# Latent attention: scores and maxima two tiles ahead, three transposed tiles in a ring, value products two steps behind

## The reference

```python
def mla_mixer(h, w_in, q_norm_g, kv_norm_g, w_uq, w_ukv, w_out, cos, sin):
    proj = h @ w_in
    c_q, c_kv, k_rope, g = split(proj)                       # 256, 128, 64, 2048 columns
    q = (rmsnorm(c_q, q_norm_g) @ w_uq)                      # 16 heads x (128 + 64)
    kv = (rmsnorm(c_kv, kv_norm_g) @ w_ukv)                  # 16 heads x (128 + 128)
    for i in range(S // 128):                                # 8 tiles of 128 queries
        q0, k_end = i * 128, (i + 1) * 128
        s = (q_nope[q0:k_end] . k_nope[:k_end] + q_rope[q0:k_end] . k_rope[:k_end]) * scale
        p = softmax(where(causal, s, -inf))                  # over i + 1 blocks of 128 keys
        outs.append(p @ v[:, :k_end])
    return (o * silu(g)) @ w_out
```

## Time and profile before

| | |
|---|---|
| median of 3 timed runs | 2548.24 us (2547.0 to 2550.31) |
| the profiled execution, own time | 2545.83 us |
| its span, first to last instruction | 2544.1 us |
| mean granted TensorE clock | 0.979 |
| PE busy | 2343.1 us, 92% |
| DVE busy | 1572.1 us, 62% |
| ACT busy | 1338.4 us, 53% |
| POOL busy | 486.3 us, 19% |

### The profile page before, as it was taken

The page is one execution under the profiler, slowest core; times in us unless marked ns, Lnnn a source line. Parts: engine busy times, 40 slices in busy tenths (PEclk is TensorE's granted clock), DMA queues, the critical chain, the costliest instruction groups (busy, mean ns, idle before and its releaser), DMA issues. The chain is left out here.

```text
span 2544.1 us, 43259 instructions
## 1 busy us (share of the span) xinstructions
PE 2343.1 (92%) x17364; PEld 1324.1 (52%) x17364; DVE 1572.1 (62%) x2220; ACT 1338.4 (53%) x2013; POOL 486.3 (19%) x434
## 2 busy tenths in 40 slices
PE   8999998988788888988897899999999999999987
PEld 4667663444444445544453455554555446776643
DVE  5566675776656656655566566666665665667764
ACT  4444443445554445454543677777778643444442
POOL 0000111122112011111032133322332520011011
PEclk9999999998899999999999999999999999999999
DMA  3011112214333334343341211112111221111013
GB/s 118 26 43 43 42 37 89 73 48 83 75 79 80 87 65 90 72 90 77 91 102 52 65 43 49 52 51 59 43 46 39 75 68 35 40 46 34 35 61 122
DMA packets 198682, 160.32 MB, mean 63 GB/s; under 512 B 160306, under 2 KB 163122, under 8 KB 198484
## 3 DMA queue, kind: packets, MB, share of 16 engines
q1 hardware_dynamic: 194388, 153.36, 22.6%
q0 software_dynamic: 4096, 4.20, 0.7%
HBM read 98.79 MB, written 4.19 MB: 40 GB/s over the span
## 5 line engine op out<-in xcount | busy, mean ns | idle before, releaser
L240 PE MATMUL psum<-h_hi,w_hi 128*128 128x512 f16 x1128 | 429.9, 381 | 35.7 <-ACT mla_silu_g L285 18.5
L242 PE MATMUL psum<-h_hi,w_lo 128*128 128x512 f16 x1128 | 429.8, 381 | 0.0
L241 PE MATMUL psum<-h_lo,w_hi 128*128 128x512 f16 x1128 | 429.5, 381 | 0.0
L2408 DVE SCALAR_TENSOR_TENSOR w_lo<-wf,w_hi 128x1024 f16<-128x1024 f32 (+3 forms) x194 | 233.5, 1212 | 137.0 <-ACT w_hi L2403 137.0
L256 PE MATMUL psum<-w_hi,h_hi 128*128 128x128 f16 x1504 | 258.0, 220 | 0.0
L257 PE MATMUL psum<-w_lo,h_hi 128*128 128x128 f16 x1504 | 257.6, 220 | 0.0
L258 PE MATMUL psum<-w_hi,h_lo 128*128 128x128 f16 x1504 | 257.5, 220 | 0.0
L1681 ACT ACTIVATE ssum<-psum,mla_neg_top 128x128 f32<-128x128 f32 (+7 forms) x128 | 94.7, 740 | 298.3 <-DVE mla_neg_top L1588 298.3
L1140 POOL TENSOR_TENSOR sb_al<-sb_zc,sb_ah 128x256 f16<-128x256 f32 (+2 forms) x96 | 166.7, 1736 | 372.2 <-ACT sb_ah L1102 372.2
L2403 ACT ACTIVATE w_hi<-wf 128x1024 f16<-128x1024 f32 (+3 forms) x194 | 187.1, 975 | 41.9 <-PE psum L242 24.5
L240 PEld LDWEIGHTS psum<-h_hi,w_hi 128*128 128x128 f16 x1128 | 110.6, 98 | 156.6 <-issue 39.7
(11 more groups left out here) (332 smaller groups left out, 5839.5 us busy)
## 6 DMA issues: line engine op xcount, KB each, us to landing
wf<-in_gla_out SPq DMA_DIRECT2D x32, 512.0 KB, 3.5
wf<-in_sb_in SPq DMA_DIRECT2D x32, 512.0 KB, 3.5
wf<-in_mla_out SPq DMA_DIRECT2D x20, 512.0 KB, 3.6
wf<-in_gla_v SPq DMA_DIRECT2D x16, 512.0 KB, 3.5
wf<-in_gla_g SPq DMA_DIRECT2D x16, 512.0 KB, 3.5
wf<-in_mla_gate SPq DMA_DIRECT2D x16, 512.0 KB, 3.8
wf<-in_sb_out SPq DMA_DIRECT2D x16, 512.0 KB, 3.5
xT<-in_x_T SPq DMA_DIRECT2D x16, 256.0 KB, 5.3
```

The source lines that it names most:

```text
L240: pe.matmul(out, wh[:, w], act_hi[:, k, tok], start=(i == 0), stop=False)
L241: pe.matmul(out, wh[:, w], act_lo[:, k, tok], start=False, stop=False)
L242: mm = pe.matmul(out, wl[:, w], act_hi[:, k, tok], start=False, stop=(i == last))
L2408: dve.scalar_tensor_tensor(out=self.w_lo[s % Layer.NSPLIT][:, 0:cols], in0=self.wf[s % Layer.NLOAD][:, 0:cols], scalar=W_SCALE, in1=self.w ...
```

## The change

The loop of the latent layer is put in another order. Scores and maximum of a tile are listed two tiles ahead instead of one. The exponential becomes an item of its own, `e`, behind the division `d` of the tile before it. The value product is listed two steps behind instead of one, right behind the scores, and the gap that stood between them moves behind it. The prologue does scores and maximum of tiles 0 and 1. The two buffers of transposed tiles become one of 21 x 256 columns, in which each tile takes what its width needs, at a place given by a table; a transpose waits for the value product of tile t - 3 instead of t - 2. The buffers of the high and low halves before the transpose stay two. No arithmetic changes.

```diff
--- before.py
+++ after.py
@@ -1209,7 +1209,7 @@
             self.qr = sb("qr_stack", [P, 4, T], F16)
             self.prob = net.ssum
             self.ph = [sb(f"prob_halves{i}", [P, 2 * T], F16) for i in range(2)]
-            self.pt = [sb(f"prob_halves_T{i}", [P, 2 * T], F16) for i in range(2)]
+            self.pt = sb("prob_halves_T", [P, self.TURNED * 2 * P], F16)
             self.cq_hi, self.cq_lo = sb("cq_hi", [P, 2, T], F16), sb("cq_lo", [P, 2, T], F16)
             self.ckv_hi, self.ckv_lo = sb("ckv_hi", [P, 1, T], F16), sb("ckv_lo", [P, 1, T], F16)
             self.kr_hh, self.kr_ll = sb("kr_hh", [P, T], F16), sb("kr_ll", [P, T], F16)
@@ -1228,7 +1228,7 @@
             self.cm = [t[:].bitcast(F32) for t in self.ph]
             self.cr = [yh[:, 3 * T:4 * T], yl[:, 3 * T:4 * T]]
 
-            self.kt = [t[:].bitcast(F32)[:, c * HALF:(c + 1) * HALF] for t in self.pt for c in range(2)]
+            self.kt = [self.pt[:].bitcast(F32)[:, i * HALF:(i + 1) * HALF] for i in range(4)]
 
             self.gate, self.split = Gate(L), Split(L)
             self.resid = Residual(L, [self.rt[0][:], self.rt[1][:]], pool_half=0,
@@ -1266,6 +1266,7 @@
     END = [("gu", 0, 0), ("gw", 2), ("gu", 0, 1), ("gu", 1, 0), ("ns", 1)] + [("nk", 1, k) for k in range(KD)] + [
         ("gu", 1, 1), ("gu", 2, 0), ("gu", 2, 1), ("gu", 3, 0), ("gu", 3, 1), ("gl", 3), ("gl", 4)]
     OUT_CLOSES = 5
+    TURNED, TURNED_AT = 21, (20, 12, 15, 8, 0, 15, 8, 0)
     ORDER = "uuuuuugrgr", "uuguuguuxrxrxx"
     def pe_cost(self, item):
 
@@ -1360,7 +1361,7 @@
         items += [("w", s) for s in range(3, 7)]
         L.split_early = range(4, 1000)
         last = MLA_HEADS * TT - 1
-        items += [("s", 0), ("m", 0), ("d", 0)]
+        items += [("s", 0), ("m", 0), ("e", 0), ("s", 1), ("m", 1), ("d", 0), ("e", 1)]
         main, filler = [], []
         for t in range(last + 1):
             h, i = divmod(t, TT)
@@ -1373,13 +1374,15 @@
             elif i == TT - 1 and h + 1 < MLA_HEADS:
                 items += weave_even(main, L.cut(filler, ("x", "g")), self.pe_cost)
                 main, filler = [], []
-            main += [("s", t + 1), ("m", t + 1), ("gap", 1)] if t < last else []
-            main += [("pv", t - 1)] if t else []
+            main += [("s", t + 2), ("m", t + 2)] if t + 2 <= last else []
+            main += [("pv", t - 2)] if t >= 2 else []
+            main += [("gap", 1)]
             main += [("d", t + 1)] if t < last else []
+            main += [("e", t + 2)] if t + 2 <= last else []
             if h % 2 and h + 1 < MLA_HEADS and 1 <= i < 5:
                 main += self.stage_items(h + 1, range(2 * i - 2, 2 * i))
             main += [("gap", 1)]
-        main += [("gap", 2), ("pv", last)]
+        main += [("pv", last - 1), ("gap", 2), ("pv", last)]
         items += weave_even(main, filler, self.pe_cost)
         early, tail = L.open_early(L.cut(self.last_out(1), ("x",)), 2)
         items += early + [("ns", 0)] + tail
@@ -1417,6 +1420,11 @@
     def gate_out(self, n):
         h, c = self.L.units[n][1]
         return self.sg[:, h % 2, c * HALF:(c + 1) * HALF]
+
+    def turned_at(self, t):
+
+        at = self.TURNED_AT[t % TT] * 2 * P
+        return self.pt[:, at:at + 2 * (t % TT + 1) * P]
 
     def pair(self, t):
 
@@ -1497,7 +1505,7 @@
                 pe.wait_ge(self.yt_ready, t // 4)
             out = L.bank(4)[:, (i % 4) * P:(i % 4 + 1) * P]
             for j in range(i + 1):
-                hi, lo = (self.pt[t % 2][:, k * P:(k + 1) * P] for k in (j, i + 1 + j))
+                hi, lo = (self.turned_at(t)[:, k * P:(k + 1) * P] for k in (j, i + 1 + j))
                 vh, vl = self.v_hi[:, h % 2, j, :], self.v_lo[:, h % 2, j, :]
                 pe.matmul(out, vh, hi, start=(j == 0), stop=False)
                 pe.matmul(out, vl, hi, start=False, stop=False)
@@ -1669,7 +1677,7 @@
             if which == "q" and p >= 1:
                 act.wait_ge(self.stacked[(p - 1) % 2], 256 * ((p - 1) // 2 + 1))
             act.activation(hi, s, ACT.Copy).then_inc(self.rhi, 1)
-        elif kind == "m":
+        elif kind == "e":
             t, = a
             w = (t % TT + 1) * P
             k = slice(t % 4, t % 4 + 1)
@@ -1766,9 +1774,9 @@
             t, = a
             w = (t % TT + 1) * P
             sp.wait_ge(self.pl_ready, t + 1)
-            if t >= 2:
-                sp.wait_ge(self.pv_done, t - 1)
-            sp.dma_start_transpose(self.pt[t % 2][:, 0:2 * w].rearrange("p (j q) -> p j q", q=P),
+            if t >= 3:
+                sp.wait_ge(self.pv_done, t - 2)
+            sp.dma_start_transpose(self.turned_at(t).rearrange("p (j q) -> p j q", q=P),
                                    self.ph[t % 2][:, 0:2 * w]).then_inc(self.turned[t % 2], 16)
 
 
```

## The result

The changed kernel takes 2571.89 us (median of 4 runs, 2569.12 to 2572.58), against 2548.45 us before (4 runs, 2547.0 to 2550.31): a ratio of 1.009, 95% interval 1.0078 to 1.0102. It is 23 us slower where 41 us faster was forecast. The profiled execution has a span of 2570.8 us and a mean granted clock of 0.973.

The account below looks back on a forecast made before the run. PE was taken to bound the kernel, with DVE-ACT pacing heads 0 to 3 about as much. Terms 19.5 + 25.6 - 3.7 = 41.4 us off the profiled 2545.8 gave 2504.4, or 2506.8 us as median; range 2470 to 2541.

Parts of the forecast that it names:

- The removed wait: PE's waits for transposes in the attention loop: all 43.7 us go, 18.1 in heads 0 to 3 and 25.6 after.
- Exponential behind the divisions: In each tile step, the ACT-DVE string of 3.7 us fits 5.6 or 6.3 us; fillers' copies come no later.
- (a): At the gate unit's PSUM bank, the later value product makes no difference; at the ends 1 us a head, 12 us.
- The step on DVE's pace: In heads 0 to 3, DVE's wait for the exponential goes: 178.7 - 18.2 = 160.5 us, for 180.
- The sum by parts: Heads 0 to 3 give 19.5 us, heads 4 to 15 give 25.6, less 3.7 at tile 123: 41.4 us.
- The clock: In heads 0 to 3 the low level costs at most 19.8 us; fewer stops lessen it, capped by DVE.
- (b): Value units of heads 1 to 3: ACT's copy stands an estimated 2.4 us, covered by the earlier exponential.
- (c): Head 15, tile 3 (t = 123): the output unit behind the value product stops PE for 3.1 to 4.3 us, taken as 3.7.
- The other two signs of being wrong: The prediction is wrong if DVE's wait for ACT's high half grows or the untouched layers behind move.
- The rule I set aside: By a skill's example, deeper buffering gains nothing here (2548 us); set aside because 43.7 us of DMA waits remained.
- B: Rival: scores wait for the exponential, over 10 us; gain only 17 us, 2531 us; chance 0.20.
- D: Rival: slower, since ACT's in-order wait for the gated output holds the gate's bank; 2557 at 3.3 us more a head; chance 0.07.

Follow-up runs that it names:

- run 3: The changed kernel, with the planner keeping the gate's copy and the rotary item with their unit when a gap ends between them: 2545.62 us.
- run 9: The changed kernel with only the exponential moved, that of tile t + 1 to the front of step t, behind the maximum of t + 2: 2528.27 us.
- run 8: The changed kernel with the exponential moved to the front of the step, and gate copy and rotary item kept with their unit: 2486.46 us.
- run 1: The kernel before, in its old order, with only the ring of three transposed tiles added: 2548.39 us, ratio 1.0002.
- run 12: run 8 without the look-ahead: scores and maximum one tile ahead, their exponential right behind, value product still two steps behind: 2571.13 us.
- run 2: The changed kernel with the staging items of odd heads listed behind the step's second gap, not in front of it: 2572.07 us.
- 10: run 8 with the last head's output projection opened one step later: 2483.88 us.
- 11: run 10 with the staging items also listed behind the second gap: 2483.20 us.

## Why the prediction was wrong

The changed kernel and the three that differ from it in nothing but the place of the exponential and the kept items put the two causes in a table (medians, us):

| | not kept | kept |
|---|---|---|
| exponential behind the division | 2571.9 (the change) | 2545.6 (run 3) |
| exponential in front | 2528.3 (run 9) | 2486.5 (run 8) |

*The removed wait.* All 43.7 us of waits for the transposes went, as forecast, and the ring by itself costs nothing (run 1), as forecast. That the order was what made the tile late held too.

*The step that failed first: "Exponential behind the divisions".* It was priced at nothing, since the string of 3.7 us fits a step of 5.6 or 6.3 us. The comparison was wrong. Every engine walks the list in its order, so it is not enough that the string fits: for as long as ACT stands in front of the exponential for DVE's low half, no unit's copy behind it frees a bank, and PE has three. The sentence "ACT waits for a low half in place of a maximum, so fillers' copies behind it come no later" compared the length of two waits and not what PE has to do meanwhile. The stop of 3.04 us shown above, 1.04 in run 9, is this case. With the two gaps joined, PE has nothing but units for those banks, but joined gaps are no cost by themselves: run 8 has them too. Moving that one item is worth 43.6 us without the kept items (2571.9 - 2528.3) and 59.1 with them. The look-ahead was under-sized beside this: without it run 8 loses 85 us (run 12) and ACT's wait for the maximum is back. That this wait is what the 85 us are made of is likely and not shown apart.

*The step that failed second: (a), "The gate", "I take no difference".* The bound was 1 us a head either way. Measured are stops of 5.83 and 0.73 us in alternate heads, where before they were 1.8 and 1.4 us, and behind the second gate unit 3.04 and 1.95 us, where before there was one of 0.9 in two heads. By the sums of all gate stops, 70.2 for 23.0 us, that is some 3 us a head more. Two links were missing from the sum, and both come from where the items fall, not from durations. The planner ended its gap between the gate unit and its copy, so the copy came a division and an exponential later; and a rotary copy had slipped behind the staging items, so ACT waited for GpSimd, for which the sum has no term. Keeping them with their unit gives 26.3 us back (run 3) and 41.8 with the exponential in front. The GpSimd link alone, 1.7 us of 5.83, is worth nothing measurable (run 2), and PE's clock is where it went.

*The step on DVE's pace, 178.7 - 18.2 = 160.5 us.* DVE's wait for the exponential did fall, from 18.2 to 1.9 us, but the remaining waits were not constants. They were waits for ACT, and ACT was late for a new reason. A sum of waits by releaser is no budget from which one row can be struck. Nor did 106.5 + 72.2 = 178.7 of 180 us show that DVE set the pace: busy time and waits fill the span of any engine, and PE's 150.4 us busy and 29.4 of waits fill the same 180.

*The sum by parts.* Heads 0 to 3 were to give 19.5 us and gave 7, most of it the shift of the cut. Heads 4 to 15 were to give 25.6 and lost 28 up to tile 120, 18 of standing and 10 of slower work.

*The clock.* I looked for a higher clock in heads 0 to 3 and it came, 0.94 for 0.88 up to tile 32. But it fell from 0.99 to 0.95 where there had been little to lose, and PE's busy time for the same matmuls grew by 10 us there. The term was counted on one side of the change only.

*(b) and (c).* The value units cost a stop of ACT of at most 2.1 us, as covered. The stop behind tile 123 was taken as 3.7 us, between 3.1 and 4.3; it is 3.38. The other two signs of being wrong did not show: DVE's wait for ACT's high half is 119.6 us over the loop, from 120.8, and what comes behind the loop takes the same time within 2 us.

*The rule I set aside.* The ring alone gave 1.0002, with 44.1 us of waits for the transposes still in the loop. So the third tile was no gain by itself, and my answer to the rule, that waits for DMA were still there to be won by depth, was no answer: those waits were the order's. Beside this stands the sentence of the Trainium skill that the prediction cites ("TensorE: Matmul & The Clock Gate", on HAM oscillation), that more buffering gave no further gain; run 1 agrees with its outcome, though not with its premise.

*The rivals.* B, scores waiting for the exponential, was marked at over 10 us: it is there with 12.2 us, nearly all in heads 0 to 3, and is the smaller part. D had the right place, the gate's bank, the right sign and nearly the right price: 3.3 us more a head, against some 3 with the unnamed stops counted in. Its link was only part of it: ACT's wait for the gated product did grow, from 20.5 to 59.5 us, but it was not what came last. It was given 0.07. What none of them had was the three-bank queue behind ACT as a whole. The 44 us of unnamed waits at units are that queue, and runs 8 and 9 show it by making them go (0.7 + 2.4 and 7.2 + 0.7 us inside the loop).

The best orders found, runs 8, 10 and 11, which can't be told apart, are 2.4 to 2.5% faster than the kernel before. Run 8 has the same items as the change, with the exponential in another place and two kinds of items kept with their unit.

## What to carry to other kernels

When an item moves in an in-order queue, the price is not its length against the step, but what stands behind it while it waits, and for how long the consumer of that has other work; here three PSUM banks. After a planner has been fed a changed list, read the list it makes, item by item around each resource that is handed over: gate copies that came an exponential late, some of them cut off from their unit, took 47 us more of PE's time, as much as the removed stall of 43.7. A wait without a named releaser can often be read off the timeline by what ended just before it. And look-ahead and distance are not to be priced one by one: here the same later value product cost 29 us or gained 26.

## What was unexpected of the hardware

Shortening a stop by 1.7 us, from 5.83 to 4.15, in five heads changed the total by nothing (2571.89 and 2572.07 us). Over the loop PE's stops fell by 9.5 us and its busy time rose by 9.6, with a granted clock of 0.94 for 0.95.

Where it went can be seen. In both kernels PE also stands 3.04 us behind each second gate unit of every other head. Of the four such stops between 916 and 1244 us, taken with the 10 us around them, none has a low clock behind it in the changed kernel, and all four have in run 2; here one, first the changed kernel, then run 2:

```profile
1022.00:1032.00 10.00, 6.96 (x68) 4.71 (x66) 4.10 (x8) 6.30 (x11) 0.00 (x0) 1.00 0.24 46
```

```profile
1022.00:1032.00 10.00, 6.96 (x43) 3.46 (x41) 5.01 (x9) 6.63 (x11) 0.00 (x0) 0.83 0.17 33
```

PE is busy equally long; the granted clock is 1.00 or 0.83. And part of the low level can fall into the stop itself, where it costs nothing: of the long stop that ends at 906.81 us, 1.8 us before 905 and as much again up to its end. So what a stop costs in clock does not follow from its own length; two stops of 3.04 us in the same place cost nothing and some 1.7 us (0.17 of 10 us). Which of the two it is, no run here explains.
